# Sparse group's logits in one TensorE visit, its value products in another

## The chip, the cores and the metric

The kernel runs on one core of a Trainium2 chip. The metric is the device time of one launch in microseconds (us); a run's time is that of its only core. The engines are TensorE (PE, with its weight loads listed apart as PEld), VectorE (DVE), ScalarE (ACT), GpSimd (POOL) and SyncE (SP); each works through its own list of instructions in order, and semaphores tie the lists together.

## The reference

Two layers over one sequence of 256 tokens with 1024 features in fp32. Cut to one layer:

```python
z = rmsnorm(x) @ w_in                      # columns: QA KA VA IDX GA (group A), QB KB VB GB (group B)
oa = sparse attention(QA, KA, VA)          # 8 heads of 64; a query keeps the 64 keys the indexer ranks best
ob = differential attention(QB, KB, VB)    # 4 heads; softmax(Q1K1) - lam * softmax(Q2K2), head-wise rmsnorm
y = concat(oa * silu(GA), ob * silu(GB)) @ w_out
x = x + rmsnorm(y)
x = x + rmsnorm((p @ w_ple_proj) * sigmoid(x @ w_ple_gate))
```

The change touches the sparse group alone: its logits (Q times K), its softmax, the transposed probabilities, and their products with VA.

## The kernel before, in words

The 256 tokens are two blocks b = 0 and 1 of 128 rows. Every projection is cut into chunks (KB, VB, QA, KA, VA, GB, GA, then the output projection WO and the gate WG), a chunk into four units of 256 rows of the weights. ACT rounds a unit's raw weights to `w_hi` (L596, called at L637), DVE forms the rest `w_lo` (L835). One unit for one block is a **piece**: six matmuls (L1233 to L1235: high by high, high by low, low by high) of 512 columns, accumulated in one of the PSUM banks `proj0` to `proj3`. There are four further banks: `sc0`, `sc1`, `tr` and `pv`.

The attention is spread in between. `layer_steps` writes one list of steps for a layer; all five engines walk this same list, and each issues only what it has to do for a step. The table `PLACE` (L75 on) says behind which piece a step stands. Pieces 0 to 55 are counted from the first of KB; VA is pieces 32 to 39, GB 40 to 47, GA 48 to 55, and in each chunk the first four are block 0. Steps at the same piece go by `rank`: gate of GB (`glu`), value product (`PV`), transposed probabilities (`PT`), transposed keys or queries (`T`), logits (`S`), exponentials (`E`), and so on, but `PV` 3 goes behind `E`. The weight preparation (`w_hi`, `w_lo`) of later units is hung on pieces as well, at the piece and ahead of its steps, two pieces per unit or a little less.

A **visit** here is one break in TensorE's stream of pieces, with all that TensorE issues for the steps behind that piece.

For the sparse group the steps are:

- `S` 3 (block 0: 16 matmuls of 128 columns, from `qT` and `kT`, L1166), `S` 4 and 5 (block 1: 24 matmuls of 256 columns each in pairs of 64 rows, three products `k_hi q_hi`, `k_lo q_hi`, `k_hi q_lo`). TensorE issues `S` 5 with `S` 4 (`S_WITH`). `S` n gives tasks i = 2n and 2n + 1, one bank each: `sc0`, `sc1` for `S` 3 and 4, `proj2`, `proj3` for `S` 5.
- On DVE the step `S` reads the bank, adds the mask, takes the maximum and writes `probs` (L986). A task needs the exponentials of the task two before it, and the transposes that read its slot of `probs`, four tasks back.
- On ACT the step `E` takes the exponentials of its two tasks (L732): eight of 128 columns for `E` 3, four of 256 columns for `E` 4 and for `E` 5.
- `PT` 3 to 8: four transposes on TensorE into `tr` (L1375), copied out by ACT (L596) to three slots of `pT` in turn, and for 8 to `kT`. A `PT` waits on TensorE for the copy of the `PT` before it (`wait_tr`) and for its exponentials.
- `PV` 3, 4, 5 on TensorE into `pv` (L1396, 16 matmuls each), copied out by ACT as `y_mix[1]`.
- `R` on DVE: reciprocals of the row sums.

ACT also has the gates: `glu` at 46 takes the sigmoid of GB's block 0 (L618), and the last piece of GB's block 1 (piece 47) and of GA's blocks (51 and 55) take theirs on ACT at once at that piece. DVE multiplies them in (L850 to L866). ACT walks its list in order: for the stretch from `PT` 4 on, this is its list in the kernel before, with the `w_hi` of units 36 to 43 in their places:

```
36 at 41 | PT4 at 41 | E4, copy PV3 at 42 | 37, E5 at 43 | 38 at 44 | PT5 at 45 | 39, glu, PT6 at 46 |
gate GB1 at 47 | 40 at 48 | 41, PT7 at 50 | 42, gate GA0, PT8, y at 51 | copy PV5, y at 52 | 43 at 53
```

The last `y` steps at 51 and 52 transpose the mixed outputs (L1314) for WO, whose pieces begin with 56.

Of the kernel before, what the change touches and what calls it, by code (L numbers as in the profile page):

```python
# [21 lines left out]
DEPTH, SEQ, D_MODEL, D_PLE = 2, 256, 1024, 256  # L22
P = 128
# [35 lines left out]
for _i, _u in enumerate(UNITS):  # L59
# [18 lines left out]
    KB=[9, 12],  # L78
    QA=[25, 29],
    KA=[32, 37],  # L80
    S=[12, 15, 18, 34, 42, 43],
    E=[13, 16, 24, 36, 42, 43],
    R=[16, 16, 19, 19, 24, 24, 40, 43, 44, 44, 44, 45],
    PT=[19, 23, 26, 40, 41, 45, 46, 50, 51],
    PV=[20, 25, 28, 42, 52, 52],
    glu=46,
    hv=[21, 27],
    hn=[23, 29],
    topk=[[0, 0, 2, 6, 6, 7, 10, 11], [12, 24, 24, 25, 26, 26, 27, 31]],
    y=[51, 52, 53])  # L90

S_WITH = {1: 2, 4: 5}


def layer_steps(L):
# [61 lines left out]
    for b in range(NB):  # L157
# [1 line left out]
    placed += [(PLACE["y"][0], ("t8", "y", 0, 1)), (PLACE["y"][1], ("t8", "y", 0, 0)), (PLACE["y"][2], ("ylo", 0))]  # L159
    rank = {"glu": 0, "PV": 1, "PT": 2, "T": 3, "S": 4, "E": 5, "hv": 6, "hn": 7, "R": 8, "topk": 9,  # L160
            "lam": 10, "t8": 11, "ylo": 12}
    for i, step in sorted(placed, key=lambda q: (q[0], 5.5 if q[1] == ("PV", 3) else rank[q[1][0]], q[1][1:])):
        mid[i].append(step)
    for c, chunk in enumerate(["KB", "VB", "QA", "KA", "VA", "GB"]):
        mms(chunk, one(0) + one(1), dict(enumerate(mid[c * len(both):(c + 1) * len(both)])))
# [51 lines left out]
def build(nc, x, p, pre_norm_g, w_in, w_out, post_norm_g, lambda_q1, lambda_k1, lambda_q2, lambda_k2, subln_g,  # L217
# [6 lines left out]
    with ctx:  # L224
# [197 lines left out]

        def s_bank(i):

            return proj[2 + i % 2] if i // 2 in S_WITH.values() else sc[i % 2]

        def pt_slot(n):

            return kT[:, :, :] if n == 8 else pT[:, n % 3, :, :]

        T8_BASE = dict(h=0, y=4, x=8)

# [161 lines left out]
        def _(act):  # L594
# [29 lines left out]
            for pos, (L, s) in enumerate(STEPS):  # L624
# [96 lines left out]
                elif kind == "D":  # L721
                    for i in range(4):
                        b, odd = divmod(i, 2)
                        act.wait_ge(dots_done, L * 4 + i + 1)
                        nc.scalar.activation(probs[:, i, 0:2 * P * (b + 1)], dots_of(b, odd), ACT.Relu,
                                             scale=HEAD ** -0.5 * IDX_HEADS ** -0.5).then_inc(relu_done, 1)
                elif kind == "E":
                    for i in (2 * s[1], 2 * s[1] + 1):
                        g, b, maps, keys = s_task(i)
                        act.wait_ge(max_done, L * 12 + i + 1)  # L730
                        for j, m in enumerate(maps):
                            last = nc.scalar.activation(probs[:, i % 4, j * keys:(j + 1) * keys],  # L732
                                                        probs[:, i % 4, j * keys:(j + 1) * keys], ACT.Exp,
                                                        bias=neg_max[:, i % 2, j:j + 1], scale=-1.0,
                                                        accum_out=row_sum[:, g, b, m:m + 1])
                        last.then_inc(exp_done, 1)
                elif kind == "PT":
                    n = s[1]
                    act.wait_ge(tr_done, tr_index(L, s))
                    if 3 <= n < 8:  # L740
                        act.wait_ge(pv_done, L * 6 + PV_OF_PT[n - 3] + 1)
                    copy(pt_slot(n).rearrange("p t q -> p (t q)"), tr[:, :]).then_inc(tr_out, 1)
                elif kind == "PV":
                    for g, b, members in PV_GROUP:
                        if g == 0 and s[1] == members[-1]:
                            act.wait_ge(pv_done, L * 6 + members[-1] + 1)
                            act.wait_ge(mix_done, L * 3 + (1 if b == 0 else 3))
                            for h in range(B_HEADS):
                                last = nc.scalar.activation(y_mix[0][b][:, h, :], pv[:, h * P:(h + 1) * P],
                                                            ACT.Square, scale=row_rec[:, 0, b, 2 * h:2 * h + 1],  # L750
                                                            accum_out=ssq_h[:, b, h:h + 1])
                            last.then_inc(sqh_done, 1)
                        elif g == 1 and s[1] == members[-1]:
                            act.wait_ge(pv_done, L * 6 + members[-1] + 1)
                            copy(y_mix[1][b], pv[:, :].rearrange("p (j t) -> p j t", j=4)).then_inc(pv_out, 1)
                elif kind == "post0":
                    b, n = s[1:]
                    wait_sum(act, L, "WO", n, b)
                    if b == 1:
                        act.wait_ge(sq_done[1], L * 4 + n + 1)  # L760

                    nc.scalar.activation(gate[:, n, :], proj[bank_of("WO", n, b)][:, :], ACT.Square,
                                         scale=D_MODEL ** -0.5, accum_out=ssq[:, 1, b, n:n + 1]).then_inc(sq_done[1], 1)
                elif kind == "ple0":
                    b, n, M = s[1:]
                    wait_sum(act, M, "WG", n, b)
                    half = work[:, b, n * N:(n + 1) * N]
                    nc.scalar.activation(half, proj[bank_of("WG", n, b)][:, :], ACT.Sigmoid).then_inc(wg_sig, 1)  # L768
                elif kind == "psq":

                    b, n, M = s[1:]
                    half = work[:, b, n * N:(n + 1) * N]
                    act.wait_ge(e_done, M * 4 + 2 * b + n + 1)
                    if 2 * b + n:
                        act.wait_ge(sq_done[2], M * 4 + 2 * b + n)
                    nc.scalar.activation(gate[:, 1, :], half, ACT.Square, scale=D_MODEL ** -0.5,
                                         accum_out=ssq[:, 2, b, n:n + 1]).then_inc(sq_done[2], 1)
                elif kind == "last" and s[1] == 0:

                    for q in range(2):  # L780
                        act.wait_ge(tail_sum, q + 1)
                        nc.scalar.activation(tail_cols(q, work), tail_bank[q][:, 0:NQ], ACT.Sigmoid)\
                            .then_inc(wg_sig, 1)
                elif kind == "last" and s[1] == 1:
                    act.wait_ge(sq_done[2], L * 4 + 3)
                    for q in range(2):
                        act.wait_ge(e_done, L * 4 + 4 + q)
                        nc.scalar.activation(gate[:, 1, q * NQ:(q + 1) * NQ], tail_cols(q, work), ACT.Square,
                                             scale=D_MODEL ** -0.5, accum_out=tail_ssq[:, q:q + 1])\
                            .then_inc(sq_done[2], 1)  # L790
                elif kind == "lam":
                    act.wait_ge(lam_sum, L + 1)
                    nc.scalar.activation(lam_e[:, :], lam_s[:, :], ACT.Exp).then_inc(lam_exp, 1)
# [298 lines left out]
        def _(pe):  # L1092
            def wait_bank(L, chunk, n, b):
# [20 lines left out]
                    pe.wait_ge(v_out, L * 4 + 2 + b + 1)  # L1114
                elif chunk == "GA":
                    pe.wait_ge(max_done, L * 12 + 12)
                elif chunk == "WO":
                    pe.wait_ge(glu_done, L * 4 + 2 * b + n + 1)
                else:
                    pe.wait_ge(wo_scaled, L * 4 + 2 * b + n + 1)  # L1120
# [65 lines left out]
            for pos, (L, s) in enumerate(STEPS):  # L1186
# [147 lines left out]
                elif kind == "D":  # L1334
# [3 lines left out]
                    for b in range(NB):  # L1338
                        keys = (b + 1) * P
                        for j in range(2):  # L1340
                            for odd in range(2):
# [3 lines left out]
                                                       start=True, stop=True)  # L1345
                                if j == 1:
                                    ins.then_inc(dots_done, 1)
                elif kind == "S" and s[1] not in S_WITH.values():
                    g, b, _, keys = s_task(2 * s[1])
                    keys_from = ("KB" if g == 0 else "KA", b)  # L1350
                    if b == 0:
# [2 lines left out]
                        pe.wait_ge(tr_out, tr_index(L, ("T",) + keys_from))  # L1354
                    if s[1] == 0:
                        pe.wait_ge(relu_done, L * 4 + 4)
                    else:
                        pe.wait_ge(max_done, L * 12 + {1: 2, 3: 4, 4: 8}[s[1]])
                    logits(L, s[1], g, b, keys)
                    if s[1] == 1:  # L1360
                        pe.wait_ge(z_out, L * 8 + 2)
                        logits(L, 2, g, b, keys)
                    elif s[1] == 4:
                        pe.wait_ge(max_done, L * 12 + 6)
                        logits(L, 5, g, b, keys)
                elif kind == "PT":
                    n = s[1]
                    g, b, tiles = pt_task(n)
# [9 lines left out]
                elif kind == "PV":  # L1378
# [2 lines left out]
                    pe.wait_ge(v_out, L * 4 + 2 * g + b + 1)  # L1381
                    if m == 0:
                        pe.wait_ge(p_lo_done, L + 1)
                    for gi, (_, _, members) in enumerate(PV_GROUP):
                        if gi and m == members[0]:
                            pe.wait_ge(pv_out, L * 4 + gi)
                    pe.wait_ge(tr_out, tr_index(L, ("PT", PV_TASKS[m][-1])))
                    for n, j, (h, kt, si, col) in [(n, j, tile) for n in PV_TASKS[m]
                                                   for j, tile in enumerate(pt_task(n)[2])]:
                        if g == 0:  # L1390
                            last = nc.tensor.matmul(pv[:, h * P:(h + 1) * P], pt_slot(n)[:, j, :],  # L1391
                                                    v_all[:, kt, 0, h * P:(h + 1) * P], start=(kt == 0),
                                                    stop=(kt == b))
                        else:
                            rows = slice(h % 2 * HEAD, (h % 2 + 1) * HEAD)
                            last = nc.tensor.matmul(pv[rows, h // 2 * P:(h // 2 + 1) * P],  # L1396
                                                    v_all[:, kt, 1, h * HEAD:(h + 1) * HEAD], pt_slot(n)[:, j, :],
                                                    start=(kt == 0), stop=(kt == b), skip_group_check=True)
                    last.then_inc(pv_done, 1)
# [30 lines left out]
```

## Time and profile before

| | us |
|---|---|
| median of 3 runs | 359.07 |
| lowest, highest | 358.68, 359.42 |
| the profiled execution | 359.26 |
| its span in the profile | 357.5 |
| PE busy in the span | 350.0 (98%) |
| DVE busy | 264.5 (74%) |
| ACT busy | 228.6 (64%) |
| POOL busy | 67.2 (19%) |

The profile's times are counted from the start of the span. PE's clock was granted at 0.997 of full over the span. Matmuls are pipelined: a matmul's own duration (0.39 us at 512 columns) is longer than the distance from its start to the next one's, and the distance is what counts for the engine's rate. In the timeline, rows of the same kind that follow each other are merged with their number behind x.

### The profile page before, as it was taken

How to read it: one execution, taken by the hardware profiler on the slowest of the kernel's cores; microseconds unless marked ns; L12 is line 12 of the kernel's file. 1: busy time of each engine (PE TensorE's matmuls, PEld its weight loads, DVE VectorE, ACT ScalarE, POOL GpSimd, SP SyncE). 2: the span in 40 equal slices, each digit the busy share in tenths (PEclk: the TensorE clock that was granted, in tenths of full speed). 3: DMA queues.
4: the chain of work that ended last, by engine and by line, in shares of the span. 5: the costliest groups of instructions: out<-in, count | busy, mean ns of one | idle time of the engine just before them, and what ended most of it. 6: DMA issues, size and time to landing. Idle time of an engine off the chain costs nothing.

```text
span 357.5 us, 5709 instructions
## 1 busy us (share of the span) xinstructions
PE 350.0 (98%) x1927; PEld 291.9 (82%) x1927; DVE 264.5 (74%) x562; ACT 228.6 (64%) x459; POOL 67.2 (19%) x121
## 2 busy tenths in 40 slices
PE   8999999999999999999999999999999999999992
PEld 7887888888888888888888888788888888888882
DVE  3886979988946766786797487988895668678543
ACT  4897557777678945555757665778658686365221
POOL 1076261142200000013106433014220000000000
PEclk9999999999999999999999999999999999999998
DMA  7996488762754454647575927556355446550011
GB/s 287 381 336 216 130 193 200 257 177 68 224 169 131 129 195 149 210 158 154 179 231 158 353 82 207 147 129 178 107 168 155 151 141 213 175 169 11 0 50 69
DMA packets 31820, 61.12 MB, mean 171 GB/s; under 512 B 2376, under 2 KB 4432, under 8 KB 31792
## 3 DMA queue, kind: packets, MB, share of 16 engines
q1 hardware_dynamic: 30656, 57.48, 50.5%
q0 software_dynamic: 1120, 3.28, 4.8%
q8 instruction: 16, 0.26, 0.3%
q14 instruction: 12, 0.10, 0.1%
q10 hardware_dynamic: 16, 0.00, 0.0%
HBM read 59.71 MB, written 1.05 MB: 170 GB/s over the span
## 4 chain that ended last, share of the span: by engine, by line
PE 96%; issue 2%; DVE 1%; ACT 0%; POOLq 0%; DVEq 0%; POOL 0%
PE proj L1233 26%; PE proj L1235 25%; PE proj L1234 25%; PE sc L1314 3%; PE tr L1375 2%; PE sc L1166 2%; PE tr L1332 2%; PE pv L1396 2%; PE pv L1391 1%; PE proj L1177 1%; PE proj L1150 1%; PE proj L1166 1%; PE proj L1246 1%; PE proj L1139 1%; PE sc L1184 1%
## 5 line engine op out<-in xcount | busy, mean ns | idle before, releaser
L1233 PE MATMUL proj<-w_hi,act_hi 128*128 128x512 f32 (+1 forms) x392 | 157.4, 402 | 0.0
L1235 PE MATMUL proj<-w_hi,act_lo 128*128 128x512 f32 (+1 forms) x392 | 152.2, 388 | 0.0
L1234 PE MATMUL proj<-w_lo,act_hi 128*128 128x512 f32 (+1 forms) x392 | 151.6, 387 | 0.0
L835 DVE TENSOR_TENSOR w_lo<-raw,w_hi 128x1024 fp32r<-128x1024 f32 (+1 forms) x102 | 121.6, 1210 | 11.1 <-ACT w_hi L596 10.5
L596 ACT ACTIVATE w_hi<-raw 128x1024 fp32r<-128x1024 f32 (+2 forms) x103 | 102.5, 1022 | 2.4 <-PE proj L1235 1.8
L1235 PEld LDWEIGHTS proj<-w_hi,act_lo 128*128 128x128 f32 x392 | 73.5, 188 | 15.5
L1233 PEld LDWEIGHTS proj<-w_hi,act_hi 128*128 128x128 f32 x392 | 73.7, 188 | 14.6 <-issue 1.0
L1234 PEld LDWEIGHTS proj<-w_lo,act_hi 128*128 128x128 f32 x392 | 73.8, 188 | 12.8
L537 POOL TENSOR_TENSOR rstd<-var,minus_half 128x1 f32<-128x1 f32 x12 | 7.6, 640 | 191.6 <-DVE var L823 162.7
L732 ACT ACTIVATE probs<-probs,neg_max 128x128 f32<-128x128 f32 (+1 forms) x64 | 28.2, 444 | 6.0 <-DVE neg_max L986 6.0
L527 POOL TENSOR_TENSOR v_all<-work,rot_tab 128x128 f32<-128x128 f32 x16 | 10.6, 664 | 77.6 <-ACT work L596 77.5
L596 ACT ACTIVATE act_hi<-sc 128x512 fp32r<-128x512 f32 x20 | 11.3, 598 | 17.6 <-PE sc L1314 16.0
L596 ACT ACTIVATE pT<-tr 128x512 f32<-128x512 f32 (+1 forms) x20 | 11.4, 572 | 10.2 <-PE tr L1375 6.9
L915 DVE TENSOR_TENSOR act_lo<-sc,act_hi 128x512 fp32r<-128x512 f32 x16 | 10.4, 684 | 5.9 <-ACT act_hi L596 5.9
L934 DVE TENSOR_TENSOR k_lo<-tr,k_hi 128x512 fp32r<-128x512 f32 x8 | 5.5, 688 | 10.5 <-ACT k_hi L596 10.5
L732 ACT ACTIVATION_READ_ACCUMULATOR probs<-probs,neg_max 128x1 f32 x64 | 12.1, 189 | 0.0
L961 DVE MAX8 top<-score 128x8 f32<-128x128 f32 (+1 forms) x32 | 11.5, 358 | 0.6
L1375 PEld LDWEIGHTS tr<-ident,probs 128*128 128x128 f32 x72 | 8.8, 140 | 2.7 <-ACT pT L596 0.7
L962 DVE MATCH_REPLACE8 score<-top,score 128x128 f32<-128x128 f32 (+1 forms) x32 | 11.0, 343 | 0.0
L1375 PE MATMUL tr<-ident,probs 128*128 128x128 f32 x72 | 10.9, 273 | 0.0
L1051 DVE TENSOR_TENSOR work<-work,emb 128x512 f32<-128x512 f32 x7 | 4.8, 687 | 7.2 <-ACT work L768 7.2
L528 POOL TENSOR_TENSOR v_all<-work,rot_tab 128x64 f32<-128x64 f32 x16 | 10.1, 632 | 0.0
(209 smaller groups left out, 441.1 us busy)
## 6 DMA issues: line engine op xcount, KB each, us to landing
raw<-in_w_in_dram SPq DMA_DIRECT2D x59, 512.0 KB, 4.2
raw<-in_w_out_dram SPq DMA_DIRECT2D x16, 512.0 KB, 3.4
raw<-in_w_ple_gate_dram SPq DMA_DIRECT2D x16, 512.0 KB, 3.7
raw<-in_w_in_dram SPq DMA_DIRECT2D x7, 324.0 KB, 5.0
raw<-in_w_ple_proj_dram SPq DMA_DIRECT2D x4, 512.0 KB, 4.2
resid<-in_x_dram SPq DMA_DIRECT2D x2, 512.0 KB, 6.2
probs<-in_w_in_dram SPq DMA_DIRECT2D x2, 512.0 KB, 9.2
g_ple<-in_ple_norm_g_dram POOLq DMA_DIRECT2D x2, 512.0 KB, 7.3
```

Source lines behind the costliest of these rows:

```text
L527: nc.gpsimd.tensor_tensor(rot_a[:, 0:heads, :], view[:, :, 0:ROT], table(cos2, slice(0, ROT)), ALU.mult)
L596: return nc.scalar.activation(dst, src, ACT.Copy, scale=scale)
L732: last = nc.scalar.activation(probs[:, i % 4, j * keys:(j + 1) * keys], probs[:, i % 4, j * keys:(j + 1) * keys], ACT.Exp, bias=neg_max[:, ...
L835: nc.vector.tensor_tensor(w_lo[:, g % SLOTS, 0:nk * cols], landing(g, nk * cols), w_hi[:, g % SLOTS, 0:nk * cols].bitcast(fp32), ALU.subtr ...
L961: link(nc.vector.max(top8[:, :], score[b][:, :]))
L962: link(nc.vector.match_replace(score[b][:, :], top8[:, :], score[b][:, :], TAKEN))
L1166: ins = nc.tensor.matmul(s_bank(2 * n + odd)[:, j * keys:(j + 1) * keys], q, k, start=(part == 0), stop=end)
L1233: nc.tensor.matmul(ps, src_hi[:, b, k0 + k, :], hi, start=(first_u and k == 0), stop=False)
L1234: nc.tensor.matmul(ps, src_hi[:, b, k0 + k, :], lo, start=False, stop=False)
L1235: last = nc.tensor.matmul(ps, src_lo[:, b, k0 + k, :], hi, start=False, stop=last_k)
L1314: last = nc.tensor.transpose(sc[i % 2][:, j * P:(j + 1) * P], tile, ident[:, :])
L1375: last = nc.tensor.transpose(tr[:, j * P:(j + 1) * P], probs[:, si % 4, col:col + P], ident[:, :])
```

## The change

Steps are placed elsewhere, and what they share is given other homes. TensorE issues `S` 3, 4 and 5 in one visit behind piece 39, with `S` 3 in the banks `pv` and `tr`; on DVE, `S` 4 and 5 stand behind pieces 40 and 45, on ACT, `E` 3, 4 and 5 behind 39, 42 and 46. `PT` 3 to 6 move from 40, 41, 45, 46 to 43, 44, 46, 47. `PV` 3 moves from 42 to 52, in front of `PV` 4 and 5, into the bank `proj1`. `PT` 6, 7 and 8 are copied to `kT` and to the idle halves of `work`.

```diff
-    S=[12, 15, 18, 34, 42, 43],
-    E=[13, 16, 24, 36, 42, 43],
-    R=[16, 16, 19, 19, 24, 24, 40, 43, 44, 44, 44, 45],
-    PT=[19, 23, 26, 40, 41, 45, 46, 50, 51],
-    PV=[20, 25, 28, 42, 52, 52],
+    S=[12, 15, 18, 39, 40, 45],
+    E=[13, 16, 24, 39, 42, 46],
+    R=[16, 16, 19, 19, 24, 24, 45, 45, 47, 47, 49, 49],
+    PT=[19, 23, 26, 43, 44, 46, 47, 50, 51],
+    PV=[20, 25, 28, 52, 52, 52],
...
-S_WITH = {1: 2, 4: 5}
+S_WITH = {1: [2], 3: [4, 5]}
...
-    for i, step in sorted(placed, key=lambda q: (q[0], 5.5 if q[1] == ("PV", 3) else rank[q[1][0]], q[1][1:])):
+    for i, step in sorted(placed, key=lambda q: (q[0], rank[q[1][0]], q[1][1:])):
...
         def s_bank(i):
-            return proj[2 + i % 2] if i // 2 in S_WITH.values() else sc[i % 2]
+            if i // 2 == 3:
+                return [pv, tr][i % 2]
+            return proj[2 + i % 2] if i // 2 in (2, 5) else sc[i % 2]
...
         def pt_slot(n):
-            return kT[:, :, :] if n == 8 else pT[:, n % 3, :, :]
+            if n < 6:
+                return pT[:, n % 3, :, :]
+            if n == 6:
+                return kT[:, :, :]
+            return work[:, n - 7, 0:N].rearrange("p (t q) -> p t q", t=4)
+
+        def pv_bank(m):
+            return proj[1] if m == 3 else pv
...
-                    if 3 <= n < 8:
+                    if 3 <= n < 6:
                         act.wait_ge(pv_done, L * 6 + PV_OF_PT[n - 3] + 1)
...
-                            copy(y_mix[1][b], pv[:, :].rearrange("p (j t) -> p j t", j=4)).then_inc(pv_out, 1)
+                            copy(y_mix[1][b], pv_bank(s[1])[:, :].rearrange("p (j t) -> p j t", j=4)).then_inc(pv_out, 1)
...
+                elif chunk == "WO" and (n, b) == (1, 0):
+                    pe.wait_ge(pv_out, L * 4 + 3)
...
-                elif kind == "S" and s[1] not in S_WITH.values():
+                elif kind == "S" and s[1] not in (2, 4, 5):
...
+                    elif s[1] == 1:
+                        pe.wait_ge(max_done, L * 12 + 2)
                     else:
-                        pe.wait_ge(max_done, L * 12 + {1: 2, 3: 4, 4: 8}[s[1]])
+                        pe.wait_ge(pv_out, L * 4 + 2)
+                        pe.wait_ge(tr_out, tr_index(L, ("T", "KA", 1)))
                     logits(L, s[1], g, b, keys)
...
-                    elif s[1] == 4:
+                    elif s[1] == 3:
                         pe.wait_ge(max_done, L * 12 + 6)
-                        logits(L, 5, g, b, keys)
+                        for n in S_WITH[3]:
+                            logits(L, n, 1, 1, SEQ)
...
-                    for gi, (_, _, members) in enumerate(PV_GROUP):
-                        if gi and m == members[0]:
-                            pe.wait_ge(pv_out, L * 4 + gi)
+                    if m == 3:
+                        pe.wait_ge(glu_done, L * 4 + 2)
+                    elif m in (1, 4):
+                        pe.wait_ge(pv_out, L * 4 + (1 if m == 1 else 2))
```

Both `PV` forms then write `pv_bank(m)` in the place of `pv`. ACT's list for the same stretch is, by the new table:

```
w_hi 35, VA1 copy, E3 at 39 | 36 at 41 | E4 at 42 | 37, PT3 at 43 | 38, PT4 at 44 | 39, glu, PT5, E5 at 46 |
gate GB1, PT6 at 47 | 40 at 48 | 41, PT7 at 50 | 42, gate GA0, PT8, y at 51 | copy PV3, copy PV5, y at 52 | 43 at 53
```

## Rows read from the trace of the kernel before

**Rows 1.** The page: the chain that ended last, by engine.
```profile
PE 96%; issue 2%; DVE 1%; ACT 0%; POOLq 0%; DVEq 0%; POOL 0%
```
**Rows 2.** Timeline of PE, first layer: start us, duration us, engine, line, operation, tiles, count.
```profile
101.65 0.39 PE L1233 MATMUL proj<-w_hi,act_hi 128*128 128x512 f32 x1
...
103.01 0.60 PE L1375 MATMUL tr<-ident,probs 128*128 128x128 f32 x4
103.37 0.48 PE L1233 MATMUL proj<-w_hi,act_hi 128*128 128x512 f32 x1
...
104.84 0.60 PE L1375 MATMUL tr<-ident,probs 128*128 128x128 f32 x4
```
**Rows 3.** The same timeline at the visit of S 3.
```profile
92.81 0.39 PE L1235 MATMUL proj<-w_hi,act_lo 128*128 128x512 f32 x1
93.13 1.16 PE L1166 MATMUL sc<-kT,qT_a 64*128 64x128 f32 x16
94.22 0.50 PE L1233 MATMUL proj<-w_hi,act_hi 128*128 128x512 f32 x1
```
**Rows 4.** The same timeline at the visit of S 4, S 5 and PV 3.
```profile
106.77 0.39 PE L1166 MATMUL sc<-k_hi,q_hi 64*128 64x256 f32 x2
106.99 0.28 PE L1166 MATMUL sc<-k_lo,q_hi 64*128 64x256 f32 x2
107.11 0.28 PE L1166 MATMUL sc<-k_hi,q_lo 64*128 64x256 f32 x2
...
108.38 1.09 PE L1396 MATMUL pv<-pT,v_all 128*64 128x128 f32 x16
109.40 0.50 PE L1233 MATMUL proj<-w_hi,act_hi 128*128 128x512 f32 x1
```
**Rows 5.** The same timeline at the visit of PV 4, PV 5 and y.
```profile
125.70 1.53 PE L1396 MATMUL pv<-pT,v_all 128*64 128x128 f32 x24
...
127.60 0.66 PE L1314 MATMUL sc<-ident,gate 128*128 128x128 f32 x4
```
**Rows 6.** ACT's table loads after the first: line L618's instructions, and the timeline.
```profile
L618 ACT ACT_TABLE_LOAD  x2: 1283/1283/1283, 116.4 to 288.5; - x2
228.17 1.28 ACT L732 ACT_TABLE_LOAD   x1
```
**Rows 7.** Timeline of ACT, first layer; idle time before an instruction in brackets.
```profile
103.65 0.60 ACT L596 ACTIVATE pT<-tr 128x512 f32<-128x512 f32 x1 [1.01 <-PE tr L1375]
...
111.99 0.49 ACT L732 ACTIVATE probs<-probs,neg_max 128x256 f32<-128x256 f32 x1
...
113.96 1.04 ACT L596 ACTIVATE w_hi<-raw 128x1024 fp32r<-128x1024 f32 x1
114.91 0.57 ACT L596 ACTIVATE pT<-tr 128x512 f32<-128x512 f32 x1
115.38 1.05 ACT L596 ACTIVATE w_hi<-raw 128x1024 fp32r<-128x1024 f32 x1
116.45 1.28 ACT L618 ACT_TABLE_LOAD   x1
117.74 0.69 ACT L618 ACTIVATE gate<-proj,rstd 128x512 f32<-128x512 f32 x1
118.33 0.59 ACT L596 ACTIVATE pT<-tr 128x512 f32<-128x512 f32 x1
```
**Rows 8.** Timeline of PE, first layer: PT 6.
```profile
115.54 0.66 PE L1375 MATMUL tr<-ident,probs 128*128 128x128 f32 x4
```
**Rows 9.** Gates by line L618: duration ns min/median/max, first and last start, first and second layer.
```profile
L618 ACT ACTIVATE gate<-proj,rstd x4: 684/689/692, 117.7 to 132.4; 128x512 f32<-128x512 f32 x4
L618 ACT ACTIVATE gate<-proj x4: 585/598/606, 289.8 to 304.4; 128x512 f32<-128x512 f32 x4
```
**Rows 10.** Groups by line and form of ACT and of DVE: busy us, mean ns of one.
```profile
L732 ACT ACTIVATE probs<-probs,neg_max 128x128 f32<-128x128 f32 x32 | 12.4, 390 | 1.0 <-DVE neg_max L986 1.0
L986 DVE CUSTOM_DVE_ANT_0 probs<-sc,sel_mask 128x128 f32<-128x128 f32 x16 | 3.5, 286 | 0.0
```

More of the change, by code:

```diff
@@ L1390, in _ @@
                         if g == 0:
-                            last = nc.tensor.matmul(pv[:, h * P:(h + 1) * P], pt_slot(n)[:, j, :],
+                            last = nc.tensor.matmul(pv_bank(m)[:, h * P:(h + 1) * P], pt_slot(n)[:, j, :],
                                                     v_all[:, kt, 0, h * P:(h + 1) * P], start=(kt == 0),
@@ L1395, in _ @@
                             rows = slice(h % 2 * HEAD, (h % 2 + 1) * HEAD)
-                            last = nc.tensor.matmul(pv[rows, h // 2 * P:(h // 2 + 1) * P],
+                            last = nc.tensor.matmul(pv_bank(m)[rows, h // 2 * P:(h // 2 + 1) * P],
                                                     v_all[:, kt, 1, h * HEAD:(h + 1) * HEAD], pt_slot(n)[:, j, :],
```

## Prediction

> **What bounds the kernel now.** I read the page's chain of waits first: 96% of the span is TensorE's own work [rows 1], so the end moves by what is taken out of TensorE's stream of instructions or put into it, and by every stall put into it. Then TensorE's timeline, for the distances between starts. Six matmuls of a piece take 1.36 us (101.65 to 103.01). A visit of four transposes with the piece behind it takes 1.83 us (103.01 to 104.84): 0.36 for the visit and 1.47 for the piece, so that coming back from a visit costs 0.11 [rows 2]. Last the timeline of ACT around the gates, since the change moves most there: ACT is only 64% busy over the span, but the transposes wait for its copies, and it works its list in order. The reader is to see two things in it. The copy of PT 5 starts at 114.91 and PT 6 can start on TensorE at 115.54, when that copy is out: 0.63 from a copy's start to the next transposes [rows 7, 8]. And exponentials and sigmoids don't share a table: a load of 1.28 stands before the first sigmoid of each layer, and another before the first exponential of the second layer at 228.17 [rows 6].
>
> **What TensorE saves.** No matmul is removed; one visit per layer is. The visit of S 3 now costs 0.09 to enter (0.32 from the start of the last matmul at 92.81, against 0.23 inside a piece), 1.09 itself (93.13 to 94.22) and 0.11 to come back: 1.29 [rows 2, 3]. Inside the common visit its 16 matmuls follow each other: 1.16 from the first start to the last end, less one matmul's own 0.28, are 15 steps of 0.059, so 0.94 for 16 [rows 3, 4]. S 4, no longer first in its visit, loses the 0.10 by which its first pair is longer than the next (0.22 against 0.12) [rows 4]. That is 1.29 - 0.94 + 0.10 = 0.45. PV 3 takes 1.02 now (108.38 to 109.40) [rows 4]; in front of PV 4 and 5, whose 32 matmuls take 1.90 or 0.059 each [rows 5], its 16 take 0.95: another 0.07. Together 0.52 per layer, 1.04 for both. The trace has no visit of this composition: the least is the entry and the return alone, 0.2 per layer; the most is 0.62, if PV 4's first matmuls lose 0.10 behind PV 3 as S 4's first pair does. I take 0.52, which has a row for each part.
>
> **What the moves do to ACT.** The new order has at piece 46 the sigmoid of GB0 (a table load), the copy of PT 5, and then E 5: exponentials, so the other table again; at piece 47 the sigmoid of GB1: the sigmoid's table a third time. Before, both sigmoids came after all exponentials, with one load. So there are two more loads per layer, and E 5 with its four exponentials stands between two copies that TensorE waits for. What is queued behind them on ACT: the copy of PT 6, which PT 7 on TensorE waits for, then `w_hi` 40 and 41, then the copy of PT 7, which PT 8 waits for. I walk both engines from the start of PT 4's visit to PT 8.
>
> TensorE, if nothing holds it: PT 4, pieces 45 and 46, PT 5, 47, PT 6, 48 to 50, PT 7, 51. That is four visits with a piece (4 x 1.83) and three more pieces (3 x 1.36), 11.40 us [rows 2].
>
> ACT: the copy of PT 4 starts 0.64 after the visit (103.01 to 103.65) [rows 2, 7] and takes 0.48 until the next can start (as 114.91 to 115.38, 0.47 to 0.49); `w_hi` 39 up to the load 1.07 (115.38 to 116.45); load 1.29; sigmoid 0.59; copy of PT 5 up to the second load 0.60, its whole length; load 1.29; E 5 1.97 (111.99 to 113.96) and 0.11 more, since a load lets the instruction before it finish (1.07 against 0.95 for a `w_hi`); third load 1.29; sigmoid 0.59; copy of PT 6 0.48; two `w_hi` 2 x 0.95; copy of PT 7 until PT 8 can start 0.63 [rows 7, 8]. Sum: 0.64 + 0.48 + 1.07 + 1.29 + 0.59 + 0.60 + 1.29 + 2.08 + 1.29 + 0.59 + 0.48 + 1.90 + 0.63 = 12.93.
>
> So PT 8 comes 12.93 - 11.40 = 1.53 late in the first layer; part of it shows already at PT 7, waiting for the copy of PT 6 (12.93 less that copy's 0.48 and the two `w_hi`, 10.55, against 9.57 for TensorE: 0.98), the other 0.55 at PT 8. In the second layer a sigmoid is 0.09 shorter [rows 9], two of them 0.18, so 1.35. Behind PT 8 TensorE is in front again. Together 2.88 of stall.
>
> The load's own price is the one number the skill sees otherwise. The rows say 0.12 to finish what runs and 1.29 to the sigmoid, 1.41 for a switch [rows 7]. The Trainium skill ("ScalarE: Activation LUTs", What ACT_TABLE_LOAD costs) gives the same load, but adds a drain of some 1.38 us, 2.66 for every switch, and its section on table sets says to do all of one set before the next, which this order does not. By that figure each of the three switches in the walk would be 1.25 dearer; the sum goes by the trace.
>
> **Is ACT free at PT 4?** From the start of the common visit, S 3's banks are full after some 1.2 and DVE's four passes on the first task take at most 4 x 0.29 [rows 3, 10]. Then ACT has E 3 (8 x 0.39), `w_hi` 36, E 4 (1.97), `w_hi` 37, the copy of PT 3 and `w_hi` 38: 3.1 + 0.95 + 1.97 + 0.95 + 0.48 + 0.95 = 8.4 [rows 7, 10]. That puts it at 10.75 at most. TensorE reaches PT 4 after the visit of 2.44 (0.94, and the 1.50 that is left of S 4 and S 5 from 106.77 to 108.38 less 0.11), the return, pieces 40 to 43 (5.44) and 1.83, at 9.82, and ACT can copy at 10.46 [rows 2, 4]. A tie: from nothing up to 0.3 later per layer. I take nothing, because DVE's passes overlap; 0.3 stays for the range.
>
> **The other moves, costed at nothing.** The common visit waits for the low part of KA's last keys: their transposes stand behind piece 37, 3.19 ahead of it, and a copy (0.64 and 0.60) and one pass of DVE follow; if a `w_hi` came in between, the margin would be a few tenths. PT 3 waits for E 3, which ends by 5.5 at most, against 8.0. GA's first piece waits for S 5's banks: DVE reads them behind PT 4, which frees the slot of `probs`, some 3.3 us after its start, against 5.0 for TensorE. If DVE's `w_lo` passes in front took longer than 1.7 more, that would be the next stall. PV 3 waits for GB1's gate, done before the copy of PT 6 and 4 us ahead. Its copy now precedes that of PV 5, but WO needs the result only five pieces later, which covers it. The weights prepared in this stretch are first used eight pieces or more later, and DVE waits with them for ACT no longer than ACT is late. No DMA issue changes its place; SP's loads follow `w_lo` and POOL has no step here.
>
> **The sum.** 2.88 - 1.04 = +1.84. The profiled execution took 359.26, so 361.10; the median of the runs is 0.19 lower, and so is my number for it: 360.9. Each layer is slower by about 0.9.
>
> **The rivals.** The bound for no change is 0.2%, 0.7 us, about what a measurement of this kernel can tell.
>
> *Faster: ACT keeps ahead and only the saved visit shows.* The point that decides is whether ACT gets from PT 4 to PT 8 in 11.40. Without the two added switches of 1.41 it would need 10.1, and TensorE would never wait. So if an exponential behind a sigmoid needed no load, the time would be 359.07 - 1.04 = 358.0. For it: E 5 is only four short instructions and ACT has 36% idle. Against it: the load at 228.17, which comes from just this succession, sigmoid and then exponential [rows 6]. Chance 0.11.
>
> *No change: the stall is only as large as the saving.* TensorE would have to be 0.5 late per layer in place of 1.44, which one switch less, or half of each hidden, would do: 359.1, between 358.4 and 359.8. For it: the sum rests on thirteen terms in a row, and 1 us in 12.9 is what separates it from this case. Chance 0.12.
>
> *The skill's switch.* Three switches 1.25 dearer in each layer are 7.5 us: 368.4. The rows contradict it by their 1.41. Chance 0.02.
>
> *The merging brings nothing:* the visits cost by their matmuls alone and no fixed part goes. Then 359.07 + 2.88 = 362.0. Against it stand the 0.32 and the 0.22 that rows 3 and 4 show at entries. Chance 0.02.
>
> The forecast has 0.73. It runs from 360.2 (both ACT walks 0.3 shorter) to 362.2 (ACT late at PT 4 by 0.3 in both layers, and only 0.2 saved per layer). The range of 8 in 10 takes in the upper half of the case of no change: 359.3 to 362.3. Faster 0.11, same 0.12, slower 0.77.
>
> **What would show it.** In the profile after: two more table loads per layer, before exponentials and before a sigmoid; one visit less per layer, S 3's matmuls at 0.059 ahead of S 4's; PT 7 and PT 8 on TensorE starting 0.63 behind ACT's copies of PT 6 and PT 7, with holes of about 1.0 and 0.5 in front of them; all of ACT's idle time between E 3 and the copy of PT 7 gone. It would be wrong if ACT shows idle time between the copy of PT 4 and that of PT 7, if there are no loads at E 5, or if the holes stand elsewhere, at the common visit (keys late) or at GA's first piece (banks late).

## The result, and the profile after

The changed kernel took 360.75 us in the median of 8 runs (lowest 360.27), the kernel before 359.14 in 8 runs beside it. The ratio is 1.0051, with a 95% interval of 1.0031 to 1.0072: slower by 1.6 us, half a per cent. Twelve further runs of it gave 361.05, against 359.28 for the kernel before beside them, ratio 1.0041 (1.0028 to 1.0054). The forecast was 360.9, in a range of 359.3 to 362.3. Of all executions in this document a single one, of the kernel tanh below, was far off at 711 us and is left out of its interval; the median is 357.83 with it and 357.82 without.

The profiled execution took 363.13, with a span of 361.3. About 2.2 us of it lie in the first 11 us, and the change has no part in them. Weights landed late (DVE waits 1.73 for the DMA ahead of its first rounding, 0.89 in the second profile), so that TensorE's first piece starts 0.65 later than in the kernel before (6.26 against 5.61). The rest is a slow start: from 7.25 to 10.67 the matmuls of 512 columns follow each other at 0.43, where a second profile of the same kernel has them at 0.23 from 6.92 on. The run two_more below shows 0.43 as the distance at half clock, but here the trace has the granted clock at full, so the reason isn't shown. No other execution of the changed kernel was as long. From the first layer's attention on, its distances are those of a second profile (span 358.8), which stands in the table further down. So only distances are read from it, not places in the span.

The page, busy time by engine: ACT has 5.8 us more than before, 5.1 of it four loads. TensorE's 1.1 more belong to the slow start: in the second profile it is busy for 349.2, 0.8 less than before.

```profile
PE 351.1 (97%) x1927; PEld 292.9 (81%) x1927; DVE 264.2 (73%) x562; ACT 234.4 (65%) x463; POOL 68.2 (19%) x121
```

The groups by line of ACT: four loads before sigmoids (L628, which was L618) and three before exponentials (L742, which was L732), where [rows 6] had two and one. The last column is idle time ahead of them.

```profile
L628 ACT ACT_TABLE_LOAD x4 | 5.1, 1283 | 0.1
L742 ACT ACT_TABLE_LOAD x3 | 3.8, 1283 | 0.1
```

The timeline of ACT in the first layer, from the copy of PT 4 to that of PT 7. It answers to [rows 7]:

```profile
113.17 0.60 ACT L606 ACTIVATE pT<-tr 128x512 f32<-128x512 f32 x1
113.66 1.05 ACT L606 ACTIVATE w_hi<-raw 128x1024 fp32r<-128x1024 f32 x1
114.73 1.28 ACT L628 ACT_TABLE_LOAD   x1
116.03 0.69 ACT L628 ACTIVATE gate<-proj,rstd 128x512 f32<-128x512 f32 x1
116.61 0.59 ACT L606 ACTIVATE pT<-tr 128x512 f32<-128x512 f32 x1
117.22 1.28 ACT L742 ACT_TABLE_LOAD   x1
118.52 0.51 ACT L742 ACTIVATE probs<-probs,neg_max 128x256 f32<-128x256 f32 x1
...
120.61 1.28 ACT L628 ACT_TABLE_LOAD   x1
121.91 0.69 ACT L628 ACTIVATE gate<-proj,rstd 128x512 f32<-128x512 f32 x1
122.49 0.59 ACT L606 ACTIVATE kT<-tr 128x512 f32<-128x512 f32 x1
122.97 2.01 ACT L606 ACTIVATE w_hi<-raw 128x1024 fp32r<-128x1024 f32 x2
124.87 0.60 ACT L606 ACTIVATE work<-tr 128x512 f32<-128x512 f32 x1
```

No row has idle time in brackets: ACT works without a pause for the whole stretch. The copy of PT 6 (into `kT`) starts at 122.49, that of PT 7 (into `work`) at 124.87. Now TensorE at the same place, with what its idle time waited for in brackets; it answers to [rows 2, 8]:

```profile
112.53 0.60 PE L1391 MATMUL tr<-ident,probs 128*128 128x128 f32 x4
...
121.88 0.39 PE L1247 MATMUL proj<-w_hi,act_lo 128*128 128x512 f32 x1
123.14 0.66 PE L1391 MATMUL tr<-ident,probs 128*128 128x128 f32 x4 [0.86 <-ACT kT L606]
123.55 0.48 PE L1245 MATMUL proj<-w_hi,act_hi 128*128 128x512 f32 x1
...
125.52 0.66 PE L1391 MATMUL tr<-ident,probs 128*128 128x128 f32 x4 [0.33 <-ACT work L606]
```

PT 7 would have started 0.23 after the matmul at 121.88, at 122.11, and starts at 123.14; PT 8 waits once more. Both start 0.65 behind the copy that they wait for. The brackets give less than the delay (0.86 of 1.03, 0.33 of 0.50), because a matmul's own duration outlasts its distance to the next. In the view of waits these are new:

```profile
PE tr L1391 <- ACT kT L606: 1.5, 2, 0.9
...
PE tr L1391 <- ACT work L606: 0.7, 2, 0.3
```

The common visit of S 3, S 4 and S 5, in place of [rows 3, 4], and the visit of all value products, in place of [rows 5]:

```profile
102.60 0.37 PE L1178 MATMUL pv<-kT,qT_a 64*128 64x128 f32 x1
...
103.51 0.37 PE L1178 MATMUL sc<-k_hi,q_hi 64*128 64x256 f32 x2
103.71 0.28 PE L1178 MATMUL sc<-k_lo,q_hi 64*128 64x256 f32 x2
...
105.12 0.50 PE L1245 MATMUL proj<-w_hi,act_hi 128*128 128x512 f32 x1
...
127.93 1.09 PE L1413 MATMUL proj<-pT,v_all 128*64 128x128 f32 x16
...
130.71 0.66 PE L1326 MATMUL sc<-ident,gate 128*128 128x128 f32 x4
```

The logits take 2.52 (102.60 to 105.12). They wait for nothing: the keys are there. The value products take 2.78 (127.93 to 130.71) for 48 matmuls.

### The profile page after: what moved, and what is told of

It reads as the page before. It is cut to its first block and busy times, and to the rows that moved or that the text cites. A ratio compares the mean times of both kernels' runs of the same rounds, so it can differ in the third digit from the quotient of the medians.

```text
span 361.3 us, 5707 instructions
## 1 busy us (share of the span) xinstructions
PE 351.1 (97%) x1927; PEld 292.9 (81%) x1927; DVE 264.2 (73%) x562; ACT 234.4 (65%) x463; POOL 68.2 (19%) x121
## 5 line engine op out<-in xcount | busy, mean ns | idle before, releaser
L742 ACT ACTIVATE probs<-probs,neg_max 128x128 f32<-128x128 f32 (+1 forms) x64 | 28.2, 443 | 3.9 <-DVE neg_max L996 3.8
L606 ACT ACTIVATE pT<-tr 128x512 f32<-128x512 f32 (+1 forms) x16 | 9.1, 566 | 6.1 <-PE tr L1333 3.6
L742 ACT ACTIVATION_READ_ACCUMULATOR probs<-probs,neg_max 128x1 f32 x64 | 12.0, 187 | 0.0
```

Source lines behind the costliest of these rows:

```text
L606: return nc.scalar.activation(dst, src, ACT.Copy, scale=scale)
```

## The experiments

One distance per layer sums up every run: from the start of the transposes of KA's first block (piece 32) to the piece behind the last `y` transposes (piece 52), both on TensorE. It holds all that the change moves. In the kernel before these are 89.85 to 128.01 and 261.87 to 300.04. Outside the two stretches the change moved nothing: between them lie 133.86 to 133.91 in every run, and behind the second 57.4. What differs from execution to execution lies ahead of the first, which starts between 89.50 and 90.27, and at 92.02 in the slow start of the changed kernel's first profile.

| kernel | stretch, layer 1 | layer 2 | both, against before | median | before, beside it | ratio, 95% interval |
|---|---|---|---|---|---|---|
| before | 38.16 | 38.17 | | | | |
| changed | 39.10 | 38.92 | +1.69 | 360.75 | 359.14 | 1.0051 (1.0031, 1.0072) |
| changed_again | 39.09 | 38.91 | +1.67 | 361.05 | 359.28 | 1.0041 (1.0028, 1.0054) |
| gate_last | 38.00 | 37.81 | -0.52 | 358.79 | 359.22 | 0.9994 (0.9983, 1.0005) |
| exps_first | 37.70 | 37.86 | -0.77 | 358.49 | 359.22 | 0.9985 (0.9975, 0.9994) |
| tanh | 37.44 | 37.46 | -1.43 | 357.83 | 359.22 | 0.9966 (0.9953, 0.9979) |
| split | 38.14 | 38.28 | +0.09 | 359.53 | 359.22 | 1.0011 (0.9993, 1.0028) |
| two_more | 43.14 | 42.99 | +9.80 | 369.80 | 359.28 | 1.0288 (1.0261, 1.0315) |
| two_hidden | 39.11 | 38.92 | +1.70 | 360.83 | 359.28 | 1.0039 (1.0024, 1.0054) |
| pt6_later | 37.48 | 37.47 | -1.38 | 357.82 | 359.28 | 0.9948 (0.9928, 0.9968) |

### The loads, or the order?

**gate_last** puts one step behind another.

```diff
-    rank = {"glu": 0, "PV": 1, "PT": 2, "T": 3, "S": 4, "E": 5, "hv": 6, "hn": 7, "R": 8, "topk": 9,
+    rank = {"glu": 5.5, "PV": 1, "PT": 2, "T": 3, "S": 4, "E": 5, "hv": 6, "hn": 7, "R": 8, "topk": 9,
```

> The changed kernel, with the sigmoid of GB0 behind E 5 at piece 46, and nothing else moved. All exponentials then come before all sigmoids, so one table load per layer is left at this place. My theory (the added loads fill ACT's queue and hold PT 7 and PT 8): ACT goes from PT 4 to PT 8 in 3.83 (it waits for PT 5) + 0.48 + 2.08 + 1.29 + 2 x 0.59 + 0.48 + 1.90 + 0.63 = 11.87 against TensorE's 11.40, a stall of 0.47 in the first layer and 0.29 in the second; with the saved 0.52 per layer the time is 359.07 + 0.76 - 1.04 = 358.8, and PT 7 waits for nothing. A rival, that E 5's late place and not the loads holds the transposes, expects no change against the changed kernel, 360.7. A second rival, that the saved visit brings nothing, expects 359.8.

358.79 was measured, 358.8 forecast, and the hit is partly luck. The two stretches have 0.91 of stall (against tanh below) less 1.43 saved, so -0.52, where 0.76 less 1.04 was forecast, -0.28; and the kernel before took 359.22 beside this run, not 359.07. The interval holds 1: this kernel can't be told from the one before. The loads fell back to one per layer at this place. On TensorE, PT 7 waits for nothing: it starts at 120.14, 4.19 behind the first of the 18 matmuls ahead of it. The piece ahead of PT 8 takes 1.96 in the first layer and 1.78 in the second against 1.47, so 0.49 and 0.31 where 0.47 and 0.29 were expected. But this run changes the order of ACT's work along with the loads. So the next one keeps every step in place.

**tanh** gives E 5 another function.

```diff
-                                                        probs[:, i % 4, j * keys:(j + 1) * keys], ACT.Exp,
+                                                        probs[:, i % 4, j * keys:(j + 1) * keys],
+                                                        ACT.Tanh if s[1] == 5 else ACT.Exp,
```

> The changed kernel, every step in its place, but E 5 takes tanh in the place of the exponential, a function that I expect to need no other table than the sigmoid (so the probabilities of the last two tasks of the sparse group are not the reference's). This keeps the order and takes away the loads alone. My theory: the walk from PT 4 to PT 8 falls from 12.93 to 10.13, no transposes wait, 358.0. The rival, that the order of E 5 between the gates is what costs, expects 360.7 as before. If the profile shows loads at E 5 the run tells nothing.

357.83, and the loads did go: two before sigmoids and one before an exponential in all, as in the kernel before. The timeline of ACT shows E 5 where it was, between the two sigmoids, without a load on either side, and idle time ahead of the copy of PT 7:

```profile
112.23 1.28 ACT L628 ACT_TABLE_LOAD   x1
...
114.11 0.59 ACT L606 ACTIVATE pT<-tr 128x512 f32<-128x512 f32 x1
114.59 0.51 ACT L742 ACTIVATE probs<-probs,neg_max 128x256 f32<-128x256 f32 x1
...
116.56 0.68 ACT L628 ACTIVATE gate<-proj,rstd 128x512 f32<-128x512 f32 x1
...
120.23 0.60 ACT L606 ACTIVATE work<-tr 128x512 f32<-128x512 f32 x1 [0.62 <-PE tr L1392]
```

On TensorE no transposes wait; this is its whole view of waits, one line of the start:

```profile
PE sc L1197 <- DVE score L811: 1.0, 1, 1.0
```

The order is the changed kernel's, the stall is gone. So it is the loads, and this run also shows what the change is worth without them: 0.72 and 0.71 per layer.

### What a load costs, and where

**two_more** and **two_hidden** add the same two small instructions, in two places.

```diff
+            def switch_twice():
+
+                nc.scalar.activation(lam_e[:, 0:1], minus_half[:, 0:1], ACT.Exp)
+                nc.scalar.activation(lam_e[:, 1:2], minus_half[:, 0:1], ACT.Sigmoid)
...
                         gate_sigmoid(L, chunk, b)
+                        if (chunk, b) == ("GB", 1):
+                            switch_twice()
```

That is two_more; two_hidden has the call here in its stead:

```diff
                          sc[i % 2][:, :]).then_inc(at_hi, 1)
+                    if s[1:] == ("y", 0, 1):
+                        switch_twice()
```

> The changed kernel with two instructions of one column more on ACT per layer, an exponential and a sigmoid, right behind the sigmoid of GB1: two more table loads in the stretch where I say ACT's queue holds TensorE. My theory: each switch costs ACT 1.41 and each small instruction about 0.25, 3.3 per layer, all of it in the end, 360.8 + 6.6 = 367.4. By the Trainium skill's 2.66 for a switch it would be 5.8 per layer, 372.4. If ACT's queue were not what holds TensorE there, 360.8.

369.80: 8.75 over changed_again, where 6.6 was my number and 11.6 the estimate by the Trainium skill's figure. The timeline of ACT tells the first part of the difference:

```profile
120.16 0.69 ACT L633 ACTIVATE gate<-proj,rstd 128x512 f32<-128x512 f32 x1
120.86 1.28 ACT L618 ACT_TABLE_LOAD   x1
122.16 0.20 ACT L618 ACTIVATE lam_e<-minus_half 128x1 f32<-128x1 f32 x1
122.36 1.28 ACT L619 ACT_TABLE_LOAD   x1
...
123.77 0.58 ACT L606 ACTIVATE kT<-tr 128x512 f32<-128x512 f32 x1
```

From the sigmoid to the copy of PT 6 ACT needs 3.61, in place of 0.58 (121.91 to 122.49 above). So the pair costs it 3.03, a little less than my 3.3; the start of one load is 1.50 behind that of the other, with a whole small instruction in between. The Trainium skill's 2.66 for a switch ("ScalarE: Activation LUTs", What ACT_TABLE_LOAD costs) doesn't fit there; its 1.28 for the load does. TensorE's hole ahead of PT 7 grows by just this, from 5.22 to 8.24 for the 18 matmuls and the wait (5.04 to 8.07 in the second layer). That makes 6.05. The rest came from TensorE itself:

```profile
120.13 0.39 PE L1254 MATMUL proj<-w_hi,act_lo 128*128 128x512 f32 x1
124.40 0.66 PE L1398 MATMUL tr<-ident,probs 128*128 128x128 f32 x4 [3.88 <-ACT kT L606]
...
125.69 0.63 PE L1254 MATMUL proj<-w_hi,act_lo 128*128 128x512 f32 x1
126.12 0.63 PE L1252 MATMUL proj<-w_hi,act_hi 128*128 128x512 f32 x1
```

After 3.88 us without work, matmuls of 512 columns follow each other at 0.43 in place of 0.23. The stretches of the same run, with the granted clock in the column ahead of the DMA share, have it at half: 1.2 of 2.4 GHz.

```profile
118.00:124.00 6.00, 2.52 (x12) 1.74 (x10) 1.58 (x4) 5.93 (x11) 0.00 (x0) 1.00 0.28 87
124.00:126.00 2.00, 1.60 (x7) 1.41 (x8) 0.68 (x1) 2.00 (x3) 0.00 (x0) 0.74 0.00 0
126.00:128.00 2.00, 2.00 (x7) 1.50 (x7) 1.81 (x4) 2.00 (x4) 0.00 (x0) 0.50 0.19 47
```

From PT 7 to PV 3 TensorE takes 5.83 there (124.40 to 130.23), against 4.79 in changed_again, and that although changed_again waits 0.50 for PT 8 within. So the slow clock costs about 1.0 per layer net of that wait, 2.1 for both. 6.05 + 2.1 = 8.15; the two stretches alone grew by 8.13 against changed_again (4.05 and 4.08). The spans of the two profiles differ by 8.8, and the other 0.7 lie ahead of the first stretch (90.27 against 89.55), in the scatter of the start. The executions of two_more also differ in the clock: those at a mean granted clock of 0.986 or 0.987 took 369.15 to 369.46, the one at 0.981 370.13, the two at 0.976 371.03 and 371.38. So in some of them TensorE was slow for longer than in the profiled one, and that is in the median of 369.80.

> The changed kernel with the same two instructions and loads per layer, but behind the copy of the first y transposes at piece 51, where ACT next waits 1.1 us for PV 3 and then for PV 5. My theory: ACT is busy 3.3 longer per layer and the copies of PV 3 and PV 5 come up to 2 late, but TensorE needs what follows from them only five pieces later, so the end does not move: 360.8. A rival, that a table load costs wherever it stands (by stopping more than ACT), expects 367 as in the run before.

360.83, no change against the changed kernel, with the same two loads per layer:

```profile
125.47 1.28 ACT L618 ACT_TABLE_LOAD   x1
...
126.97 1.28 ACT L619 ACT_TABLE_LOAD   x1
...
128.37 0.58 ACT L606 ACTIVATE qT_a<-proj 128x512 f32<-128x512 f32 x1
128.85 0.59 ACT L606 ACTIVATE qT_a<-pv 128x512 f32<-128x512 f32 x1
```

The copies of PV 3 and PV 5 follow at 128.37 and 128.85, without the idle times of 1.1 that stood ahead of them in changed_again. TensorE's stretch is 39.11 and 38.92, as without. So a load does not stop TensorE by itself; its price is what waits for ACT at its place.

### What a visit costs

**exps_first** takes the loads away in yet another order, and **split** gives S 5's matmuls a visit of their own in it.

```diff
-    S=[12, 15, 18, 39, 40, 45],
-    E=[13, 16, 24, 39, 42, 46],
+    S=[12, 15, 18, 39, 40, 44],
+    E=[13, 16, 24, 39, 42, 45],
...
-    rank = {"glu": 0, "PV": 1, "PT": 2, "T": 3, "S": 4, "E": 5, "hv": 6, "hn": 7, "R": 8, "topk": 9,
+    rank = {"glu": 2.5, "PV": 1, "PT": 2, "T": 3, "S": 4, "E": 5, "hv": 6, "hn": 7, "R": 8, "topk": 9,
```

And split on top of it:

```diff
-S_WITH = {1: [2], 3: [4, 5]}
+S_WITH = {1: [2], 3: [4]}
...
-                elif kind == "S" and s[1] not in (2, 4, 5):
+                elif kind == "S" and s[1] == 4:
+                    logits(L, 5, 1, 1, SEQ)
+                elif kind == "S" and s[1] not in (2, 5):
```

> The changed kernel with S 5 on VectorE behind piece 44, E 5 behind 45, and the sigmoid of GB0 behind the copy of PT 5 at 46. One table load per layer is left at this place, and the copy of PT 5 stands ahead of it. My theory: no transposes wait, ACT reaches PT 8 at about 10.8 after PT 4 against 11.40, only the saving is left, and the time is 359.07 - 1.04 = 358.0. If the visits brought nothing it would be 359.1; if the added loads were not the cause of the stall, still 360.7.

> The kernel exps_first, with the matmuls of S 5 taken out of the common visit and issued in a visit of their own behind piece 40; the same matmuls, the same work on the other engines. It measures what one visit costs beside its matmuls. My theory (entry 0.09, return 0.11, a first pair 0.10 longer, a last pair 0.09 longer): 0.4 per layer, so 0.8 over exps_first, 358.8. The rival, that a visit costs its matmuls alone, expects no difference from exps_first.

exps_first gave 358.49, half a us over my number: the forecast that no transposes wait failed. PT 6, not PT 7 or PT 8, waits in it. E 5 now stands ahead of the copy of PT 5 and itself starts 0.42 late in the first layer, waiting for DVE, and TensorE's waits have, beside two of the start, a line that I had not expected:

```profile
PE tr L1391 <- ACT pT L606: 0.2, 1, 0.2
```

In the timeline the piece ahead of PT 6 takes 1.67 in the first layer and 1.79 in the second against 1.47, so 0.52 in all. The margin that I had counted on there was not enough.

split gave 359.53, 1.04 over exps_first; the two stretches, which leave out the scatter of the start, give 0.44 and 0.42 per layer, against my 0.4. Its parts are in the timeline: an entry, a longer first pair, a last one longer than its matmuls need, and the return.

```profile
103.64 0.39 PE L1247 MATMUL proj<-w_hi,act_lo 128*128 128x512 f32 x1
103.96 0.38 PE L1178 MATMUL proj<-k_hi,q_hi 64*128 64x256 f32 x2
104.19 0.28 PE L1178 MATMUL proj<-k_lo,q_hi 64*128 64x256 f32 x2
...
104.66 0.28 PE L1178 MATMUL proj<-k_hi,q_lo 64*128 64x256 f32 x2
104.86 0.50 PE L1245 MATMUL proj<-w_hi,act_hi 128*128 128x512 f32 x1
105.20 0.40 PE L1246 MATMUL proj<-w_lo,act_hi 128*128 128x512 f32 x1
```

0.32 - 0.23 to enter, 0.23 - 0.12 at the first pair, 0.20 - 0.12 at the last, 0.34 - 0.23 to return: 0.39. The same matmuls, so a visit has a price of its own, and the rival that it has none falls: the intervals of the two runs only just touch, but the stretches differ by 0.4 in both layers.

### A version faster than both

**pt6_later** is exps_first with PT 6 one piece later.

```diff
-    PT=[19, 23, 26, 43, 44, 46, 47, 50, 51],
+    PT=[19, 23, 26, 43, 44, 46, 48, 50, 51],
```

> The kernel exps_first with PT 6 behind piece 48 in the place of 47. In exps_first's profile PT 6 still waits 0.2 and 0.3 for the copy of PT 5, which stands behind E 5 on ACT. My theory: one piece later the copy is out, PT 7 has its own 0.3 us of margin left, no transposes wait, and 0.5 to 0.6 of exps_first's time goes: 357.9, or 1.2 under the kernel before. If PT 7 waits in turn, the time stays at 358.4.

357.82, ratio 0.9948 (0.9928 to 0.9968) to the kernel before and 3.2 us under the changed one beside it. No transposes wait any more; the whole view of TensorE's waits is one line of the start, as in the kernel before:

```profile
PE sc L1196 <- DVE score L810: 1.1, 1, 1.1
```

**changed_again** is the changed kernel without an edit.

> The changed kernel once more, beside the others on the same chip, for a narrower interval and a second profile. 360.8, or 1.6 over the kernel before; in the profile the holes in front of PT 7 and PT 8 again at 1.0 and 0.5 in the first layer, 0.85 and 0.5 in the second.

361.05 was measured. Its holes are at the same places: the 18 matmuls and the wait ahead of PT 7 take 5.22 and 5.04, less 4.19: 1.03 and 0.85; the piece ahead of PT 8 takes 1.97 in both layers, 0.50 more than 1.47.

## Why the prediction was right, point by point

**The end follows TensorE.** It does: the two stretches on TensorE grew by 1.69, the median by 1.61.

**The stall.** Forecast: PT 8 late by 1.53 and 1.35, split 0.98 and 0.55 in the first layer. From PT 4 to PT 8 the profile has 12.99 (112.53 to 125.52) where the thirteen terms gave 12.93, and the holes are 1.03 and 0.50. tanh, with nothing else than the loads taken away, gives the whole stall: 39.10 - 37.44 = 1.66 and 38.92 - 37.46 = 1.46. That is 0.12 more per layer than forecast, and TensorE's rows say where from: transposes that waited take longer. PT 7 takes 0.41 in place of 0.36, PT 8, with the y transposes behind it, 0.49 where it took 0.43 in the kernel before (123.35 to 123.78). The sum had left this out.

**The saving.** Forecast 0.52 per layer, measured 0.72 (tanh against before). The parts: the pieces of the stretch lost 0.32, where entry and return were put at 0.20. The other 0.12 are mainly the pieces behind PV 3 (4.26 for 18 matmuls in the kernel before, against 4.19 or 4.20 elsewhere) and a wait of 0.06 ahead of PT 6 that the kernel before had [rows 8] and this order hasn't. PT 6's own visit lost the 0.06 that such a wait adds. The logits lost 0.18 (1.09 + 1.61 to 2.52), not 0.25: S 3 takes 0.91, but S 4 and S 5 take 1.61 as before, and S 4's first pair is still long at 0.20. The value products lost 0.14 (1.02 + 1.90 to 2.78), not 0.07: inside one visit their matmuls follow at 0.058. The parts were the right ones, but the term was too small by more than a quarter.

**Both together** gave 1.69 where 1.84 was forecast: 3.12 of stall less 1.43 saved, against 2.88 less 1.04. Both terms were too small, by 0.24 and 0.39, and the errors mostly cancelled. The mechanism and the places of the holes were right; that the number came within 0.15 of the median is partly luck.

**ACT free at PT 4** was called a tie. In the profile after, the copy of PT 4 starts at 113.17, 0.64 behind its transposes, so in time; the copy of PT 3 was 0.39 late (111.72, transposes at 110.69), which TensorE didn't see.

**The rivals.** That ACT keeps ahead falls with the profile after: it has no pause in the stretch. That there is no change, the stall being only as large as the saving, falls with the 3.12 against 1.43 and with both intervals. That the merging brings nothing falls with split and tanh. The Trainium skill's dearer switch falls with the loads' rows; those of two_more, 1.50 apart with a whole instruction between, show it most directly.

**The moves costed at nothing** cost nothing: tanh has all of them and no wait is left in it. Of the new homes of S 3, of PV 3 and of the transposed tiles no run shows the price alone; what is left of them is inside the measured saving.

## What to carry to other kernels

When a step moves on one engine, write down the order of every engine that walks the same list, and look for functions of different tables that now take turns: here two loads of 1.28 us per layer turned a saving of 0.72 into a loss of 0.85. What such a load costs is decided by who waits for ACT behind it: nothing behind a copy that is needed five pieces later, all of it ahead of a copy that TensorE stands for. On a TensorE that never pauses, even a visit's fixed 0.4 us is real time, and is won only if the engines that feed it still have room for their lists.

## What the runs showed that I had not expected

A long wait of TensorE has a second price: the hole of 3.88 us in two_more was followed by about 3 us at half clock, 1.2 of 2.4 GHz, and that cost some 1 us more in each layer. The holes of 1.0 us in the changed kernel left the granted clock at full, and cost their own length and 0.06 for the transposes behind them. The Trainium skill names the gate ("TensorE: Matmul & The Clock Gate", Part 1): idle time lets the array fall to half rate, and work brings the full rate back. The run agrees, but the fall came late: the granted clock is still 1.00 all through the hole. In the second layer, after a hole of 3.72, the transposes and three matmuls of 512 columns still ran at the full rate (to 302.42), and only those behind them stood 0.43 apart.

The transposes' visit that had to wait takes 0.41 in place of 0.36, in every such place of these profiles (PT 7 in the changed kernel, PT 6 in exps_first, 0.42 there).
